# A two-block layer in one kernel: norms and linear-attention heads in token layout, a respaced weave, and moved waits and transfers

## The reference, cut to what matters

```
x1   = rms_norm(first_block(x), norm_final_g)
mod  = silu(c) @ w_ada + b_ada                       # shifts, scales, gates
h    = rms_norm(x1, norm_mix) * (1 + sc1) + sh1      # and the same for 256 context tokens
hy, q, k, v, og, gf, gb = split(h @ w_in)
# linear attention, 4 heads (key 64, value 128), forward and backward, chunks of 64 tokens
o    = intra-chunk attention + (q * exp(b)) @ state at the chunk's start
y_g  = o * rsqrt(mean(o*o over the head's 128 values) + eps) * gla_norm * silu(og)
# Hyena: short convolution, long convolution by a DFT, filter made by a small MLP
y_h  = x0 * long_conv(x1_ * v)
x2   = x1 + g1 * (concat(y_h, y_g) @ w_out)
x3   = x2 + g2 * (square(relu(h2 @ w1)) @ w2),  h2 = rms_norm(x2, norm_mlp) * (1 + sc2) + sh2
out  = rms_norm(x3, norm_final)
```

## Time and profile before

| | us |
|---|---|
| median of 3 executions | 1854.93 (1854.02 to 1858.47) |
| the profiled execution, its own time | 1860.19 |
| its span, first to last instruction | 1858.4 |
| TensorE busy | 1756.4 (95%) |
| VectorE / ScalarE / GpSimd busy | 934.2 / 666.6 / 773.1 |
| TensorE's share of the chain that ended last | 90% |
| mean granted TensorE clock | 0.966 of full speed |

### The profile page before, as it was taken

The page is one execution under the profiler, slowest core; times in us unless marked ns, Lnnn a source line. Parts: engine busy times, 40 slices in busy tenths (PEclk is TensorE's granted clock), DMA queues, the critical chain, the costliest instruction groups (busy, mean ns, idle before and its releaser), DMA issues.

```text
span 1858.4 us, 20171 instructions
## 1 busy us (share of the span) xinstructions
PE 1756.4 (95%) x7930; PEld 1370.9 (74%) x7930; DVE 934.2 (50%) x1227; ACT 666.6 (36%) x1038; POOL 773.1 (42%) x338
## 2 busy tenths in 40 slices
PE   5999999999998899999999989989978799999997
PEld 4786766678985767777767767778767588888885
DVE  5716565487233633333345674464484677162524
ACT  6124334364333434444432443541222232222222
POOL 2433222254731367877863433222032444444441
PEclk8999999999999999999999999999789899999998
DMA  5232211133630345555552234121023323333331
GB/s 180 80 91 61 65 46 51 57 119 93 181 95 19 91 125 169 160 166 167 167 167 79 77 99 126 47 57 29 17 79 114 91 80 91 103 94 98 97 96 46
DMA packets 294035, 179.85 MB, mean 97 GB/s; under 512 B 7930, under 2 KB 277780, under 8 KB 293685
## 3 DMA queue, kind: packets, MB, share of 16 engines
q1 hardware_dynamic: 292788, 172.05, 31.5%
q10 hardware_dynamic: 592, 4.39, 0.7%
q0 software_dynamic: 560, 2.12, 0.3%
HBM read 174.22 MB, written 4.32 MB: 96 GB/s over the span
## 4 chain that ended last, share of the span: by engine, by line
PE 90%; DVE 5%; ACT 2%; issue 1%; DMA 1%; POOL 0%; SPq 0%; DVEq 0%; ACTq 0%
PE ps L1033 57%; PE ps L1045 13%; PE ps L1059 5%; PE ps L1338 2%; PE ps L1200 1%; PE ps L1168 1%; PE ps L1509 1%; PE ps L1282 1%; PE ps L1180 1%; PE ps L1263 1%; PE ps L1159 1%; ACT WH L576 0%; DVE tmp L1995 0%; PE ps L1476 0%; PE ps L1492 0%
## 5 line engine op out<-in xcount | busy, mean ns | idle before, releaser
L557 POOL TENSOR_TENSOR WL<-raw,WH 128x1024 fp32r<-128x1024 f32 (+2 forms) x330 | 770.6, 2344 | 1037.8 <-ACT WH L576 1037.6
L576 ACT ACTIVATE WH<-raw 128x1024 fp32r<-128x1024 f32 (+2 forms) x330 | 331.0, 1006 | 824.8 <-PE ps L1033 650.3
L1033 PE MATMUL ps<-hH,WH 128*128 128x512 f32 x808 | 206.5, 398 | 3.7 <-POOL WL L557 1.5
L1033 PE MATMUL ps<-hL,WH 128*128 128x512 f32 x808 | 200.2, 390 | 0.0
L1033 PE MATMUL ps<-hH,WL 128*128 128x512 f32 x808 | 199.6, 389 | 0.0
L1033 PEld LDWEIGHTS ps<-hH,WH 128*128 128x128 f32 x808 | 151.0, 188 | 46.7 <-issue 8.0
L1033 PEld LDWEIGHTS ps<-hL,WH 128*128 128x128 f32 x808 | 151.5, 187 | 32.7
L1033 PEld LDWEIGHTS ps<-hH,WL 128*128 128x128 f32 x808 | 151.0, 187 | 32.2
L1045 PE MATMUL ps<-hH,WH 128*128 128x512 f32 x328 | 141.7, 432 | 4.0 <-DVE tmp L2173 3.4
L1045 PE MATMUL ps<-hH,WL 128*128 128x512 f32 x328 | 131.8, 402 | 0.0
L1045 PE MATMUL ps<-hL,WH 128*128 128x512 f32 x328 | 131.7, 402 | 0.0
(11 more groups left out here) (452 smaller groups left out, 2836.7 us busy)
## 6 DMA issues: line engine op xcount, KB each, us to landing
raw<-in_w_in_dram SPq DMA_DIRECT2D x64, 512.0 KB, 3.7
raw<-in_w_mlp_dram SPq DMA_DIRECT2D x64, 512.0 KB, 3.8
raw<-in_w_ada_dram SPq DMA_DIRECT2D x48, 512.0 KB, 3.6
raw<-in_w_gate_up_dram SPq DMA_DIRECT2D x44, 512.0 KB, 3.7
raw<-in_w_out_dram SPq DMA_DIRECT2D x16, 512.0 KB, 3.5
raw<-in_w_ckv_dram SPq DMA_DIRECT2D x16, 512.0 KB, 3.8
raw<-in_w_down_dram SPq DMA_DIRECT2D x16, 448.0 KB, 3.2
raw<-in_k_dft_dram SPq DMA_DIRECT2D x17, 256.0 KB, 2.8
```

The source lines that it names most:

```text
L557: pool.tensor_tensor(WL[un.slot][:, 0:s_.kt, 0:n], raw[un.slot][:, 0:s_.kt, 0:n], WH[un.slot][:, 0:s_.kt, 0:n].bitcast(F32), ALU.subtract) ...
L576: act.activation(WH[un.slot][:, 0:s_.kt, 0:n], raw[un.slot][:, 0:s_.kt, 0:n], ACT.Copy).then_inc(high_done, 1)
L1033: ins = pe.matmul(dst, w[un.slot][:, q, 0:m], a[:, q, :], start=(k == 0), stop=(k == 3 * kt - 1))
```

## The change

1. **Norm of the mixer.** `token_sums` puts the data in the stationary place and one column of ones in the moving place, so that the sums come out with tokens on partitions (128x4). The small vector is worked on, the root taken once for both norms, and `spread` brings it back to 128x512 in PSUM by matmuls of a broadcast column with the identity. `modulate` reads it in PSUM instead of SBUF. The norm ahead of the MLP is made so too.
2. **Last norm.** Each tile of the last stage is scaled by the gain on ScalarE and transposed by TensorE between the units; at the end the token's factor is a scalar for each partition. Four transfers of 512 KB instead of two of 1 MB.
3. **Linear attention.** `weigh_gla` swaps its operands, so the output has tokens on partitions; the head's norm is a reduction on VectorE, and four transposes replace the matmul with ones. Steps are renumbered, `ogp` 2 and 3 go behind `grp`, `silu` of og goes to step 8, and softplus and exponentials are interleaved anew.
4. **Weave.** `hyp` 2 and 3 go between the `uu` pairs; the `uu` banks become 5, 6, 3, 4.
5. **Late low wait.** `unit` waits for the high part first, and for the low part only ahead of its last eight matmuls.
6. **Filter transfers.** They are issued by ScalarE in `dn0`, nine after the first slab and the decay table after the fourth; SyncE's wait goes.

The rest renames and merges semaphores.

```diff
+WEAVE = ([("hyp", i) for i in HYP_FIRST] + [("uu", 0), ("uu", 4), ("hyp", 2), ("uu", 1), ("uu", 5), ("hyp", 3)]
+         + [("uu", i) for i in (2, 6, 3, 7)])
...
-        KEND_STEP, STATE_STEP, FB_STEP = (2, 3, 4, 5), (6, 8, 10, 12), (12, 14, 16, 18)
-        O_STEP, NORM_STEP, TURN_STEP = (14, 16, 18, 20), (16, 18, 20, 22), (18, 18, 19, 19)
+        KEND_STEP, STATE_STEP, FB_STEP = (2, 3, 4, 5), (6, 8, 10, 11), (12, 13, 15, 17)
+        O_STEP, HEAD_STEP, TURN_STEP = (14, 15, 17, 19), (16, 17, 19, 21), (17, 17, 18, 18)
+        PAIR_STEP = [1 + FILL.index((at["uu", HT + k], None)) for k in range(HT)]
...
-            sp.wait_ge(unit_done, first_u("dn0"))
...
+                if i == 0:
+                    act.dma_start(zT[:], t["k_z"]).then_inc(filt_in, 16)
...
+            def token_sums(src, c0):
+                for tt in range(ST):
+                    ins = pe.matmul(ps[:, 7, c0 + tt:c0 + tt + 1], src[:, tt * P:(tt + 1) * P], ones[:, 0:1],
+                                    start=True, stop=True, skip_group_check=True)
+                ins.then_inc(stat_sum, 1)
+            def spread(b, c0):
+                for tt in range(ST):
+                    ins = pe.matmul(ps[:, b, tt * P:(tt + 1) * P], tok_r[:, c0 + tt:c0 + tt + 1].to_broadcast([P, P]),
+                                    ident[:], start=True, stop=True, skip_group_check=True)
+                ins.then_inc(rr_mm, 1)
             def unit(un, rh, rl, n=S, m=P, extra=None):
-                pe.wait_ge(low_done, un.u + 1)
+                pe.wait_ge(high_done, un.u + 1)
...
                     for w, a in ((WH, rh_), (WH, rl_), (WL, rh_)):
+                        if w is WL:
+                            pe.wait_ge(low_done, un.u + 1)
...
-                    pe.matmul(ps[:, 2, b * P:(b + 1) * P], vG[:, b, h * P:(h + 1) * P],
-                              att[h % 2][:, b * P:(b + 1) * P], start=True, stop=True, skip_group_check=True)
+                    pe.matmul(ps[:, 2, c], att[h % 2][:, c], vG[:, b, h * P:(h + 1) * P],
+                              start=True, stop=True, skip_group_check=True)
...
-                            ins = pe.matmul(ps[:, 2, c], state[g][rows, n, :], qin[g][rows, c],
+                            ins = pe.matmul(ps[tok_rows, 2, c], qin[g][rows, n * CHUNK:(n + 1) * CHUNK], state[g][rows, n, :],
                                             start=False, stop=True, skip_group_check=True)
...
-                pe.matmul(bank(7), ones[:], o2[h % 2][:], start=True, stop=True).then_inc(gh_mm, 1)
+                for b in range(ST):
+                    c = slice(b * P, (b + 1) * P)
+                    ins = pe.transpose(ps[:, 7, c], oT[h % 2][:, c], ident[:])
...
+                    for i in range(1, DT):
+                        unit(at[name, i], mH[1], mL[1])
+                        turn_final(i - 1)
```

More of the change, by code:

```diff
@@ L359, in build @@
             elif s_.name == "hyp":
[L361 to L364, removed]
+                order += [(st[name], i) for name, i in WEAVE]
+            elif s_.name == "ogp":
+                order += [(s_, 0), (s_, 1), (st["grp"], 0), (s_, 2), (s_, 3)]
+            elif s_.name not in ("ada", "uu", "grp"):
                 order += [(s_, i) for i in range(s_.n)]
@@ L873, in _ @@
             act.wait_ge(x_ok, 1)
[L874 to L880, removed]
+            act.dma_start(x_dram[:], x[:]).then_inc(x_moved, 16)
             def soft(g):
@@ L1397, in _ @@
             unit(at["sa", 0], abH[:, 0], abL[:, 0])
-            stat("fin1", res["dn2"], DT)
-            pe.matmul(bank(6), ones[:], acc2[:], start=True, stop=True).then_inc(stat_sum, 1)
-            units("sa", abH[:, 0], abL[:, 0], S, 1)
+            pe.wait_ge(res["dn2"], DT)
+            token_sums(acc, 0)
+            token_sums(acc2, 4)
+            units("sa", abH[:, 0], abL[:, 0], S, 1, 3)
+            pe.wait_ge(tok_rr, 1)
+            spread(6, 4)
+            spread(5, 0)
+            units("sa", abH[:, 0], abL[:, 0], S, 3)
             units("sb", abH[:, 1], abL[:, 1])
             opening("qp", hH, hL, tiles(), md_ok, 2)
-            units("ogp", hH, hL)
+            units("ogp", hH, hL, S, 0, 2)
             pe.wait_ge(md_ok, 2 * DT)
@@ L1633, in _ @@
             dve.wait_ge(h_ok, DT)
-            dve.wait_ge(lam_in, 64)
+            dve.wait_ge(tables_in, 80)
             for c in range(2):
@@ L2088, in gated @@
                 dve.wait_ge(g_done, g + 1)
-            dve.wait_ge(x_out, 16)
+            for i in range(2):
+                copy_unit("ogp", 2 + i, og[:, 2 + i, :])
+                gate_in_(i)
+            sums(0)
+            copy_unit("kp", 0, kG[:, 0, :], 1.0, kGc[:, 0, :])
+            gate_in_(2)
+            sums(1)
+            copy_unit("kp", 1, kG[:, 1, :], 1.0, kGc[:, 1, :])
+            gate_in_(3)
+            sums(2)
+            keep_vp(0)
             to_edge(0)
+            sums(3)
+            keep_vp(1)
+            dve.wait_ge(x_moved, 16)
             to_edge(1)
             gated(0)
+            keep_vp(2)
             to_edge(2)
             gated(1)
+            keep_vp(3)
             to_edge(3)
```

350 lines of the change are left out of this document (187 added, 163 removed).

## The result

The changed kernel takes **1800.05 us** (median of 4, 1799.03 to 1800.06); the kernel before took 1856.64 beside it (1854.02 to 1858.47). The ratio is 0.9701 (95%: 0.9684 to 0.9717): 56.6 us faster, where 54 were predicted. In the profiled executions the span fell from 1858.4 to 1798.2, by 60.2: the profiled execution of before (1860.19) lies above its median.

| step | predicted | trace |
|---|---|---|
| 1 filter transfers, late low wait | 5.5 | 4.7 (2.9 at 659, 1.8 at the filter) |
| 2 mixer's norm | 4.5 | -0.3 |
| 3 projections | 7 | 11.3 |
| 4 heads | 10 | 18.7 |
| 5 weave | 18 | 16.3 |

A forecast was written before the change was run, and what follows sets the result against it. TensorE was taken to bound the kernel, busy 1756.4 of 1858.4 us. Seven gains summed to 54 us, from 1854.93 to 1801 us; the range leaving 2 in 10 out was 1784 to 1825.

The forecast's parts named there:

- Step 1: Filter transfers moved to ScalarE and the late low wait: stalls at the filter and at 659 go, 5.5 us gained.
- Step 2: Mixer's norm: factor ready some 6 us earlier, `qp` opens sooner and the slow clock probably goes, 4.5 us gained.
- Step 3: Projections: the idle time ahead of the first key transpose and its slow clock mostly go, 7 us gained.
- the three new waits: Projections: `grp` for the context's activations 2.3 us, key transpose for the last value tile 1.5, reset table 0.5.
- step 7: The end of the kernel: transposes between the last units, a shorter tail after them, 6 us gained.
- Step 4: Linear attention heads: swapped weighing 3.6 us, norm transposes 3, clock 5, less 1.6 for tighter waits; 10 us gained.
- Step 5: Weave of `uu` and `hyp` up to `inv`: pairs get more time and four banks, 18 us gained.
- a sign of being wrong: At `inv`: a wait of over 4 us there would show the prediction wrong.
- Steps 6 and 7: The MLP's norm, 3 us gained with its slow clock staying, and the kernel's end, 6 us gained.
- The mid-unit wait: Rival, all 224 units: 0.24 us each at the low part costs 54 us, all of the gain; chance 0.04.
- ScalarE in order: Rival: its ordered work replaces the stalls at filter, projections and weave; 17.5 us less gain, 1818 us; chance 0.17.
- The heads got clean: Rival, heads: 64-column products overlap and the clock holds, 21 us gained there, 1790 us; chance 0.14.

The follow-up runs named there:

- tiles_early: The changed kernel with ScalarE's modulate tiles placed earlier, among its copies of `sa` and `sb`: 1794.02 us.
- heads_old_steps_back: The changed kernel with the heads in their old form and on their old step numbers, all else kept: 1823.82 us.
- steps_back: The changed kernel with the heads' old step numbers; their new form and the new weave stay: 1796.87 us.
- heads_alone: The kernel before with only the heads' new form (operand order, norm, turning by transposes), on old steps and old weave: 1829.4 us.
- weave_back: The changed kernel with the old weave order and the old ring of three `uu` banks: 1804.66 us.
- filter_sync: The changed kernel with the ten filter transfers back in SyncE's order, the late low wait kept: 1796.33 us.
- order_back: The changed kernel with the old weave order alone, the ring of four `uu` banks kept: 1799.77 us.
- inv_order: The changed kernel with ScalarE making the second `inv` slab before pair 2's high parts, and VectorE's first pair 3 products before pair 2's low parts: 1792.82 us.
- low_early: The changed kernel with the wait for the low part back at the start of each whole unit: 1799.43 us.
- best: The changed kernel with the edits of filter_sync, steps_back, tiles_early and inv_order together: 1784.38 us.
- after_again: The changed kernel measured again with no edit: 1799.99 us.

## Why the prediction was right, and where it was not

- **Step 1 (5.5; 4.7).** The 3.63 us behind the slab went, the stall at 659 gave 2.9 instead of 1.5. But the landing cost 1.84 and kept the slow clock; I had 1 for it and none of the clock. I had also taken both parts as needed: either alone removes the stall, and with the late wait SyncE's place is 1.7 us better, at the clock. My test (no idle over 2 us) held.
- **Step 2 (4.5; -0.3).** The factor was ready 5.5 us earlier in the stage, as I had it (some 6). What failed is what I took to follow: that `qp` opens 2.9 us earlier. It opens 35.5 us behind the first `sa` matmul, where it was 34.9. I looked only at ScalarE's last tiles, not at where its program has the first; with the tiles moved (tiles_early) it is 32.7. And TensorE ends `sb` 3.5 us later, not 2: the small products cost 2.2, the rest is a slow clock behind the new sums (1076.0 to 1079.4) that was not there before. My test (under 3.5 us ahead of `qp`) failed with 4.49.
- **The read in PSUM** did what its row suggested. Line 2038 took 0.73 us at 1100.22 while GpSimd's subtraction ran from 1100.06 to 1102.54; line 2043 behind it, both inputs in SBUF, took 2.21. By the rule of the Trainium skill (SBUF — State Buffer, "SBUF: two separate sides") the second is shut out and the first is not; the trace agrees. What it brought in time no run shows; I had counted nothing. The same blow now falls on line 2043, and 2.21 us there stand on the way to the last `sb` copy.
- **Step 3 (7; 11.3).** The stall of 4.55 us and its clock went. Of the three new waits that I had at 4.3 us in all none shows; a wait of 0.7 for the last value tile's copy was there before, with 0.6. No kernel undoes this part alone: that the 11.3 us are its own is read from the traces, not shown by an experiment. The same holds for step 7.
- **Step 4 (10; 18.7, and 27 by experiment).** The work comes out near (6.6 predicted, 7.3 left over by the trace), but by two errors that meet: four `weigh_gla` give 6.9 us, where I had 3.6, because eight products take 0.65 us and start in pairs, and the norm gives less than the 3 I had. The clock did not: I took 5 of 13.4 back, because I put its fall down to scores and weighing standing together for 6 us. They stand so in heads_old_steps_back and in steps_back alike; at 0.82 in the one and 1.00 in the other. The form decides. Which half of it, the wide products or the norm without a 512-column sum, wasn't tried alone.
- The Trainium skill (TensorE: Matmul & The Clock Gate, "Part 4: PE-mode transpose") says that transposes don't count as busy for the clock; by that the added ones would help to lower it. Steps_back has twelve of them in its stage, 2.0 us of 49.7, at 1.00: here they did not.
- **Step 5 (18; 16.3).** The size is right and the cause mostly wrong. I gave all of it to the weave. Of the 15.4 us up to the first `inv` matmul, undoing the weave costs 6.1 (37.7 to 43.8). The new form alone takes 4.9 off this stretch (53.1 to 48.2), just what VectorE's first product starts earlier (11.7 to 6.9 us). The pair time of 7.5 us stayed as I had it; I had not asked when the first pair starts. The remaining 4.4 us (48.2 to 43.8) lie between heads_alone and weave_back, which differ in the steps and all the rest: 2.8 are again an earlier first product (6.9 to 4.0), which fits the last head's earlier steps but is not separated. With the heads late as before, the rest of the change gives 8.4 (53.1 to 44.7 in heads_old_steps_back), so weave and heads cover in part the same loss. Ahead of `inv` it waits 4.43, which I had named as a sign of being wrong.
- **Steps 6 and 7 (3 and 6; 1.5 and 7.6).** The MLP's norm keeps its slow clock (0.74) and a wait for `acc` of 4.2 us (the mixer's is 0.8). At the end the transposes cost 2.9 (3.0 predicted); the store took 6.7 us from the first issue, not 7.5, and VectorE's scalings 0.71 each, not 0.9.
- **Rivals.** The mid-unit wait costs nothing (266.82 and 266.80). ScalarE in order did take a stall's place, in step 2 and ahead of `inv`; the two experiments on it give 8.5 us by their stages. The heads got clean.

## What to carry to other kernels

A part that holds up two engines and the clock pays more than its own work: the heads' new form was worth 7 us of products, and 27 in time. Compare two traces from the start of the same work: by the start of the span the mixer's factor is ready 10.5 us earlier, by the start of its stage 5.5. When a reciprocal is taken away, look up where each engine's program has the first use of its result; the gain stops at the first engine that comes there on its own schedule. Compare stage by stage between several kernels before adding up medians: the same clock effect can stand in each of them.

## What the runs showed that I had not expected

**One and the same short wait costs 1.2 or 2.8 us.** At the second `scores_gla` (step 13) TensorE waits 1.2 us for VectorE in all kernels with the new steps and the new form. Two windows of 6 us, the wait and what follows, in the changed kernel and in filter_sync:

```profile
1262.00:1268.00 6.00, 4.79 (x27) 3.81 (x27) 3.79 (x7) 0.00 (x0) 0.49 (x1) 0.93 0.15 44
1268.00:1274.00 6.00, 6.00 (x37) 4.56 (x37) 1.64 (x3) 1.72 (x2) 1.18 (x1) 0.79 0.00 0
```

```profile
1260.00:1266.00 6.00, 4.79 (x28) 3.84 (x27) 3.79 (x7) 0.00 (x0) 0.47 (x1) 1.00 0.15 44
1266.00:1272.00 6.00, 6.00 (x50) 4.48 (x49) 2.55 (x4) 1.85 (x3) 2.36 (x1) 1.00 0.01 3
```

TensorE's instructions and the wait are the same, but 37 matmuls pass in one and 50 in the other. The heads' stage was 52.7 us in the profiles of the changed kernel, its repetition, weave_back, order_back and inv_order, and 51.2 in filter_sync, low_early and tiles_early. What decides between them, the runs don't show; where the wait is gone (steps_back, best) it is 49.6 each time. Likewise at the filter: a wait of 1.59 us with a slow clock behind it (after_again), one of 1.58 (low_early) without.
